# Experts ranked by token count: passes of two with 64 slots and of four with 32

## The reference

```python
N_EXPERTS, TOP_K, EXPERT_FF, SHARED_FF = 32, 4, 256, 512
comb = sum over the 4 chosen experts of one_hot(idx) * w        # (tokens, 32)
g = einsum("td,edf->tef", xf, w_exp_gate)                       # (32, 2048, 256)
u = einsum("td,edf->tef", xf, w_exp_up)                         # (32, 2048, 256)
a = silu(g) * u * comb
routed = einsum("tef,efd->td", a, w_exp_down)                   # (32, 256, 2048)
out = routed + (silu(xf @ w_sh_gate) * (xf @ w_sh_up)) @ w_sh_down
```

## Time and profile before

| | us |
|---|---|
| median of 3 runs | 1325.61 (1323.4 to 1325.62) |
| span of the profiled execution | 1322.1 |
| PE busy | 1222.6 (92%) |
| VectorE busy | 517.6 (39%) |
| ScalarE busy | 227.0 (17%) |
| moved by DMA | 379.59 MB, 287 GB/s over the span |

### The profile page before, as it was taken

The page is one execution under the profiler, slowest core; times in us unless marked ns, Lnnn a source line. Parts: engine busy times, 40 slices in busy tenths (PEclk is TensorE's granted clock), DMA queues, the critical chain, the costliest instruction groups (busy, mean ns, idle before and its releaser), DMA issues.

```text
span 1322.1 us, 16803 instructions
## 1 busy us (share of the span) xinstructions
PE 1222.6 (92%) x6125; PEld 655.8 (50%) x6126; DVE 517.6 (39%) x1058; ACT 227.0 (17%) x482; POOL 8.7 (1%) x13
## 2 busy tenths in 40 slices
PE   2789999999999899989979999999999999999974
PEld 0435588888744544457834444444334444444421
DVE  1200487656267588542532222222223332222215
ACT  4210200000125400040011111111111111111103
POOL 0000000000000000000000000000000000000001
PEclk9989999999999999989989999999999999999988
DMA  9999989996574499763549999945999999999951
GB/s 341 345 354 335 315 297 366 350 326 219 163 278 141 151 343 387 274 243 128 181 145 361 344 344 345 347 156 162 348 348 346 350 349 357 343 345 346 347 198 63
DMA packets 276337, 379.59 MB, mean 287 GB/s; under 512 B 12674, under 2 KB 182864, under 8 KB 274640
## 3 DMA queue, kind: packets, MB, share of 16 engines
q1 hardware_dynamic: 276304, 379.14, 84.1%
HBM read 377.01 MB, written 2.10 MB: 287 GB/s over the span
## 4 chain that ended last, share of the span: by engine, by line
PE 88%; DVE 3%; DMA 3%; issue 2%; SPq 2%; ACT 1%; POOL 0%; POOLq 0%; DVEq 0%; ACTq 0%
PE ps L485 85%; DMA ring<-in_w_mod 3%; DVE nreg L1619 1%; PE ps L855 1%; SPq L311 1%; PE ps L778 0%; SPq L303 0%; DVE tiny L1386 0%; PE ps L555 0%; DVE nreg L1623 0%; PE ps L730 0%; PE ps L872 0%; ACT nreg L928 0%; PE ps L500 0%; ACT nreg L1049 0%
## 5 line engine op out<-in xcount | busy, mean ns | idle before, releaser
L485 PE MATMUL ps<-nreg,ring 128*128 128x256 f32 (+1 forms) x1280 | 301.0, 395 | 10.2 <-ACT nreg L928 5.8
L485 PEld LDWEIGHTS ps<-nreg,ring 128*128 128x128 f32 x1280 | 244.0, 192 | 63.9 <-issue 21.8
L485 PE MATMUL ps<-ring,nreg 128*64 128x512 f32 x1088 | 241.2, 602 | 0.0
L1239 DVE SCALAR_TENSOR_TENSOR part<-ring,csT,part 128x512 f32<-128x512 f32 x240 | 180.4, 752 | 9.2
L1619 DVE TENSOR_TENSOR nreg<-nreg,ps 128x512 f32<-128x512 f32 x136 | 87.4, 684 | 176.2 <-PE ps L485 176.2
L485 PEld LDWEIGHTS ps<-ring,nreg 128*64 128x64 f32 x1088 | 77.5, 139 | 151.9 <-issue 151.9
L485 PE MATMUL ps<-nreg,conv 128*128 128x512 f32 x272 | 134.9, 618 | 13.5 <-DVE nreg L1619 13.5
L485 PE MATMUL ps<-ring,conv 128*64 128x512 f32 x544 | 128.0, 602 | 0.5 <-ACT conv L928 0.5
L485 PE MATMUL ps<-ring 128*128 128x512 f32 x256 | 110.8, 592 | 0.0
L485 PEld LDWEIGHTS ps<-nreg,conv 128*128 128x128 f32 x272 | 46.0, 189 | 101.5 <-DVE nreg L1619 60.2
L485 PE MATMUL ps<-pick,qnT 128*128 128x128 bf16 x544 | 93.2, 220 | 1.1 <-issue 0.6
(11 more groups left out here) (193 smaller groups left out, 753.1 us busy)
## 6 DMA issues: line engine op xcount, KB each, us to landing
ring<-in_w_mod SPq DMA_DIRECT2D x88, 1024.0 KB, 9.4
ring<-in_w_exp_gate SPq DMA_DIRECT2D x128, 512.0 KB, 8.2
ring<-in_w_exp_up SPq DMA_DIRECT2D x128, 512.0 KB, 8.6
ring<-in_w_exp_down SPq DMA_DIRECT2D x128, 512.0 KB, 8.6
ring<-in_w_in SPq DMA_DIRECT2D x15, 2048.0 KB, 11.9
ring<-in_w_out SPq DMA_DIRECT2D x8, 2048.0 KB, 10.9
ring<-in_w_mod SPq DMA_DIRECT2D x4, 2048.0 KB, 19.8
ring<-in_w_sh_up SPq DMA_DIRECT2D x2, 2048.0 KB, 10.2
```

Of the source, the lines that this page charges most:

```text
L485: return nc.tensor.matmul(o, l, r, start=start, stop=stop)
L1239: ins = V.scalar_tensor_tensor(out=acc, in0=w, scalar=scale, in1=acc, op0=ALU.mult, op1=ALU.add)
```

## The change

- VectorE and PE rank the experts by token count on the chip (`order`, largest first; ties by number). The counts are compared with each other expert's; a transpose and two matmuls permute places, weights and counts into ranked order. `order` is stored as integers, and SP reads the numbers of the experts of a pass into registers and loads their weights.
- The 16 heaviest experts go in 8 passes of two with 64 slots, the 16 lightest in 4 passes of four with 32 slots. The order is four rounds of: pair, pair, four. Each main pass has its own skipped or repeated `extra_passes` before it, so PE's loop over three rounds holds six pass bodies, and six stand behind it for the last round.
- In a pass of four the gate and up weights are eight units through four slots, the down weights four units through two slots.
- Channel order in the expert stage: chunk 4q + j, partition p is channel 512q + 4p + j. Four consecutive rows of gate and up weights lie in one partition, packets of 4 KB. Down weights are loaded in halves of 1024 columns, 4 KB too. The router and shared weights, the modulation columns, the norm's gain and the transposed tokens follow the same order: shared loads are four DMAs each, `bT2` and `fnT` are loaded apart in runs of four floats, `xh` is written from a strided read, and `mod_sum_cols` has a strided weight operand.
- The routing work moves in front of the split of the tokens on VectorE and among the first shared products on PE.

The core of the diff:

```diff
-        wg = w_exp_gate[0].rearrange("e (c p) n -> p e c n", p=P)
+        wg = w_exp_gate[0].rearrange("e (q p j) n -> p e q (j n)", q=4, j=4)
...
+            for at, src in ((bT2[:, 0:KC], b_mod[0, 3 * D:4 * D]), (bT2[:, KC:2 * KC], b_mod[0, 4 * D:5 * D]),
+                            (fnT[:, :], ffn_norm[0])):
+                sp.dma_start(at.rearrange("p (q j) -> p q j", q=4), src.rearrange("(q p j) -> p q j", q=4, j=4))\
+                  .then_inc(cols_in, 16)
...
+            def load_unit(v, q, experts):
+                for u, e in enumerate(experts):
+                    for g, src in ((0, wg), (1, wu)):
+                        sp.dma_start(gu[v][:, u, g, :, :].rearrange("p k n -> p (k n)"),
+                                     src[:, bass.ds(e, 1), q, :].rearrange("p a x -> p (a x)")).then_inc(gu_in[v], 16)
...
+            for i in range(ROUNDS):
+                quarters, halves = 12 * i, 6 * i
+                if i:
+                    for q in range(2, 4):
+                        sp.wait_ge(quarter_used, quarters - 2 + q // 3)
+                        load_unit(q, q, pair)
+                    for h in range(2):
+                        sp.wait_ge(half_used, halves)
+                        load_down(h, h, pair)
+                pair = [expert_at(4 * i + 2), expert_at(4 * i + 3)]
+                for q in range(4):
+                    sp.wait_ge(quarter_used, quarters + q + 1)
+                    load_unit(q, q, pair)
+                for h in range(2):
+                    sp.wait_ge(half_used, halves + h + 1)
+                    load_down(h, h, pair)
+                four = [expert_at(HEAVY + 4 * i + u) for u in range(4)]
+                for q in range(4):
+                    for g in range(2):
+                        v = 2 * q + g
+                        sp.wait_ge(quarter_used, quarters + (v + 5 if v < 4 else 8 + (v - 4) // 2 + 1))
+                        load_unit(v % 4, q, four[2 * g:2 * g + 2])
+                for g in range(2):
+                    sp.wait_ge(half_used, halves + g + 3)
+                    load_down(g, 0, four[2 * g:2 * g + 2])
+                if i + 1 < ROUNDS:
+                    pair = [expert_at(4 * i + 4), expert_at(4 * i + 5)]
+                    for q in range(2):
+                        sp.wait_ge(quarter_used, quarters + 11)
+                        load_unit(q, q, pair)
+                for g in range(2):
+                    sp.wait_ge(half_used, halves + 5)
+                    load_down(g, 1, four[2 * g:2 * g + 2])
...
+            def gate_up(units, use, wide, t, last):
+                for q in range(4):
+                    for g in range(units):
+                        v = units * q + g
+                        pe.wait_ge(gu_in[v % 4], 64 * use + 64 * (v // 4))
+                    pe.wait_ge((gx_act, gx_dve)[q % 2], 2 * t + (q // 2 + 1))
+                    for k in range(4):
+                        for u in range(2 * units):
+                            w = gu[(units * q + u // 2) % 4]
+                            ins = mm(ps[wide * u:wide * u + wide, 2, :], xg[:, 4 * q + k, wide * u:wide * u + wide],
+                                     w[:, u % 2, :, k, :], q == 0 and k == 0, q == 3 and k == 3)
...
-            with pe.Fori(0, NE // 2 - 1) as i:
-                extra_passes(i)
-                pair_pass(i, pe.snap(passes, min_val=0, max_val=64), True)
-                pe.reg_add(passes, passes, 1)
-            extra_passes(NE // 2 - 1)
-            pair_pass(NE // 2 - 1, pe.snap(passes, min_val=0, max_val=64), True, ahead=False)
+            with pe.Fori(0, ROUNDS - 1) as i:
+                for n in range(2):
+                    extra_passes(2 * i + n, PASSES - 1, 1, 4 * i + (n + 1))
+                    main_pass(1, 4 * i + (n + 1))
+                extra_passes(i + 8, NPASSES - 1, 2, 4 * i + 3)
+                main_pass(2, 4 * i + 3)
+            last_round = 4 * (ROUNDS - 1)
+            for n in range(2):
+                extra_passes(last_round // 2 + n, PASSES - 1, 1, last_round + n + 1)
+                main_pass(1, last_round + n + 1)
+            extra_passes(8 + ROUNDS - 1, NPASSES - 1, 2, last_round + 3)
+            main_pass(2, last_round + 3, ahead=False)
```

More of the change, by code:

```diff
@@ L70, in constants @@
     c[:, C_HALF] = -0.5
+    for p in range(P):
+        c[p, C_TIE:C_TIE + NE] = np.arange(NE) > p % NE
+        c[p, C_BLK + p // NE] = 1.0
+        c[p, C_EXP] = p % NE
+    c[:, C_OFF:C_OFF + NPASSES] = NARROW * np.arange(NPASSES)
     return c
@@ L131, in block_kernel @@
         xh = slot[3].rearrange("p (t d) -> p t d", t=2)
-        gu = ring[:, 0:16384].rearrange("p (q u g k n) -> p q u g k n", q=4, u=2, g=2, k=4)
-        down = [slot[4 + u].rearrange("p (k n) -> p k n", k=2) for u in range(2)]
+        gu = [slot[v].rearrange("p (u g k n) -> p u g k n", u=2, g=2, k=4) for v in range(4)]
+        down = [slot[4 + v].rearrange("p (u k n) -> p u k n", u=2, k=2) for v in range(2)]
+        tbl = vrow[:, :].rearrange("p (a e) -> p a e", a=4)
+        tblT = brow[:, :]
+        heavy = crow[:, :].rearrange("p (n t r) -> p n t r", n=PASSES, t=2)
+        blocks, sums = part[:, 1, 0:128], part[:, 1, 128:192]
         wkr = kq[:, 0:1024].rearrange("p (k n) -> p k n", k=KC)
@@ L847, in _ @@
-            gather(0, (2, 3))
-            def pair_pass(i, t, last, ahead=True):
+            for m in range(2):
+                shared_up(0, 0, sh_gate, m)
+            pe.wait_ge(mask_ready, 1)
+            mm(ps[:, 5, 0:32], before, mask[:, 0, :], True, True)
+            mm(ps[:, 5, 32:64], ones, mask[:, 0, :], True, False)
+            mm(ps[:, 5, 32:64], before, mask[:, 1, :], False, True)
+            mm(ps[:, 5, 64:96], ones, mask[:, 0, :], True, False)
+            mm(ps[:, 5, 64:96], ones, mask[:, 1, :], False, True).then_inc(rank_full, 1)
@@ new lines, in _ @@
+            shared_up(1, 2, sh_up, 0, range(8))
+            pe.wait_ge(sort_in, 1)
+            nc.tensor.transpose(ps[:, 6, 0:128], vrow[:, :], ident).then_inc(tbl_full, 1)
+            shared_up(1, 2, sh_up, 0, range(8, KC))
+            pe.wait_ge(tbl_out, 1)
+            mm(ps[:, 7, 0:128], tblT, blocks, True, True)
+            mm(ps[:, 7, 128:192], ones, sums, True, True).then_inc(sort_full, 1)
+            shared_up(1, 2, sh_up, 1)
+            pe.wait_ge(rank_ready, 1)
+            pe.wait_ge(sh_act, 2)
@@ L853, in pair_pass, with expert_pass @@
+            def expert_pass(units, use, t, last, ahead=True):
+                wide = P // (2 * units)
                 pe.wait_ge(pickw_ready, t + 1)
@@ L1587, in weighted_picks @@
[L1587 to L1592 removed]
+            heavy_slots = heavy.rearrange("p n t r -> p (n t r)")
+            light_slots = light[:, :, :, :].rearrange("p n t r -> p (n t r)")
```

353 lines of the change are left out of this document (203 added, 150 removed).

## The result

The changed kernel takes 1419.12 us (median of 4 runs, 1418.62 to 1421.12) against 1325.06 us (1323.4 to 1325.62): ratio 1.0716, 95% interval 1.0701 to 1.0732, slower by 94 us. The profiled execution took 1421.12 us with a span of 1419.3 (before 1322.1).

The account below looks back on a forecast made before the run. TensorE was taken to bound the kernel, the DMA nearly as full. Stage -26.2, stalls +92.4 and front +5.8 made +72.0 us; with the 1322.1 us span and 3.5 us around it 1398 us, range 1340 to 1420.

Parts of the forecast that it names:

- The stalls: TensorE's expert loop: 11 jumps over skipped repeats cost 8.4 us each, 6.2 idle plus slower clock; +92.4 us.
- the two jumps back: End of each turn of TensorE's new loop: between 0 and 6 us each, taken at nothing.
- The sign in the instruction queue: Profile after: the queue moves more packets than 22, by more than the added code.
- The reading of the two gaps: Kernel before, TensorE idle 6.83 us at loop entry, 5.82 behind it: jumps into code not held cost some 6 us.
- Rival (b): TensorE's jumps over a body cost nothing, the next code comes ahead of the jump: 1305 us, chance 0.20.
- The stage without stalls: Expert stage: nine passes of two 325.5 us, three fours of 70.0, a last of 65.8; 601.3 against 627.5, -26.2 us.
- Sum 70.0 us: A pass of four with a successor: 4.0 us to first request, 2.3 to bytes, ten units 51.1, then TensorE's remaining work.
- The front: Ahead of the expert stage: column loads, router packets, extra products, strided reads and weight loads; +5.8 us, range 0 to 13.
- the strided weight loads in the modulation sums: Front, eight groups of 8 records at 0.95 us each: between 0 and 7.6 us more, taken as 2.
- Rival (c): Packets don't matter, DMA stays at 349 GB/s: +34 us to any case, 1432 with the forecast; chance with (d) 0.05.
- Rival (d): The chip's ranking leaves a light expert with over 32 tokens; not in the sum, chance with (c) 0.05.
- SP's reads and VectorE's picks: Expert stage: SP's reads of 34 expert numbers and VectorE's 16 picks for a four are covered; nothing.

Follow-up runs that it names:

- experiment 3: The kernel before with TensorE's expert stage written straight, the repeat only ahead of the sixth pair, no skips: 1302.17 us, ratio 0.983.
- Experiments 9 and 10: experiment 3 with a test ahead of 13 later passes, jumping over a never-run body: 48 records in the first, 1301.86 us; 400 in the second, 1389.52 us.
- Experiment 1: The kernel before with TensorE's expert loop of two pass bodies written as a loop of four: 1450.88 us, ratio 1.096.
- Experiment 4: The changed kernel with TensorE's stage written straight, the repeat only ahead of the first pass, no skips: 1325.03 us, ratio 1.000.
- Experiment 5: Experiment 4 with the six ring slots given to gate/up and down units alike, in order of use: 1246.32 us, ratio 0.941.
- experiment 7: Experiment 4 with the channels laid out as in the kernel before, 1 KB packets for gate and up: 1332.64 us, ratio 1.007.
- experiment 8: experiment 3 with the experts' gate and up weights read in 4 KB packets, tokens not laid out to match: 1302.4 us.
- experiments 6 and 11: Experiment 5 plus a general second version with repeats, behind one test; TensorE reads eleven counts in the first, 1254.94 us, one VectorE sum in the second, 1244.03 us.

## Why the prediction was right

The forecast was 1398 us with 1340 to 1420, and the median is 1419.12: the direction and the cause held, and the time came out 21 us above the forecast. That it is still in the range is by 0.9 us, so partly luck: the stage's other errors all went one way.

- **The stalls: right in number, and by some luck in sum.** 11 x 8.4 = 92.4 us was the term, 94.1 is what taking the jumps out returned. Its parts were less exact. The idle time was 70.1 us against 11 x 6.2 = 68.2, but two errors meet in it: a jump ahead of a four costs 2.9 to 3.4 us and not 6.2, and the two jumps back, which I put at nothing, make their gaps 13.4 us, some 7 us more than a skip alone. The slower clock adds the rest. The sign in the instruction queue came too: the 8 bodies more (4160 records) are some 17 packets by the counts of experiment 3, an estimate, and the queue moved 45 more. Behind the gap at 763.91 the window of the changed kernel shows the same lower level as the earlier trace rows:
```profile
770.00:775.00 5.00, 4.54 (x12) 1.49 (x14) 1.75 (x8) 0.38 (x1) 0.00 (x0) 0.54 0.02 7
```
- **The reading of the two gaps, confirmed and made narrower.** That code which isn't at hand costs, and not the jump, was read from the earlier trace rows against the earlier trace rows. Experiments 9 and 10 show it directly, and show that it hangs on the distance. Rival (b), that the code behind a jump comes ahead of it, is true of 48 records and not of 400 or of a pass. (The pass period that the prediction gives as 36.17 us is 36.13 by its own two rows; nothing hangs on it.) The rule of the Trainium skill ("Runtime: NRT & Kernel Launch", Instruction fetch mechanics) is that a taken jump which lands outside what was prefetched waits for a fetch; experiments 9 and 10 agree with it. The same section gives TensorE's store 2048 instructions. Experiment 1 shows less: a loop of four bodies, 4 x 424 = 1696 matmul and weight-load records, isn't held. With the waits and register instructions beside them four bodies are some 1810 instructions, an estimate from experiment 3's 23 more packets for 13 more bodies, at 256 instructions a packet.
- **The stage without stalls: too optimistic by 17.7 us.** I had -26.2 us. Experiment 4 has 1307.74 - 688.72 = 619.0 us from the first gather's end to the last scatter's, against 627.5 before: -8.5. The failed term is a four, "Sum 70.0 us": the three with a successor take 72.8, 74.5 and 72.8 (+10.1 in all), the last 71.9 in place of 65.8 (+6.1), and the nine pairs 1.3 more in all. The rate was right, 410 to 412 GB/s. What was wrong is how many bytes go ahead of the last ones. In the first four of experiment 4 the last down weights were to land 57.4 us in (4.0 + 2.3 + 51.1); TensorE's products on them start 60.1 us in, and what follows takes 12.7 us, as in the sum (12.6):
```profile
842.63 0.35 SPq L448 DMA_DIRECT2D ring<-in_w_exp_gate  x1
...
856.64 3.64 PE L551 MATMUL ps<-ring,conv 128*32 128x512 f32 x16 [15.56 <-issue]
...
796.50:856.64 60.14, 28.91 (x266) 11.81 (x265) 7.55 (x21) 5.36 (x13) 0.00 (x0) 0.79 0.94 367
808.00:856.64 48.64, 21.53 (x199) 9.69 (x200) 4.45 (x11) 4.98 (x12) 0.00 (x0) 0.75 1.03 410
```
367 GB/s over 60.14 us are 22.07 MB, where ten units are 20.97. The 1.1 MB more are 2.7 us at 410 GB/s, all that is missing; SP issues the next pair's third and fourth quarters from 842.63 us on, while the last down units are still on their way, and the sum had left these out. In the last four three steps are longer: the first half's down weights come 1.7 us later, their products take 1.6 us more at the lower clock, and the last two down units 16.2 us in place of 12.5, with part of the final norm's gain among them. The end is 0.9 us shorter.
- **The pairs behind the fours.** They take 39.4 and 36.5 us in experiment 4, and part of it is not TensorE's own. Its gather waits for VectorE's picks, 2.05 us behind the first four and 0.58 behind the second:
```profile
885.61 0.29 PE L551 MATMUL ps<-pick,qnT 128*128 128x128 bf16 x1 [2.05 <-DVE pick L1717]
```
Ahead of these picks VectorE, whose program still has its loop and its skips, stands idle for 7.63 us at its loop's jump back and 4.23 us at the skip behind it, put down to no other engine. That it is the same stall as TensorE's is likely and not tested.
- **Where the gain of four passes fewer went.** Not into jumps alone. Without them the kernel still is no faster than before, because the fours wait for their weights: the ring holds half a four, and the pair passes before it can't load ahead, since slots are reserved, four for gate/up and two for down. Experiment 5 moved nothing but the slots and the order of the loads, and gained 78.7 us.
- **The front: 11.0 us by experiment 7 against 5.8.** The failed term is the strided weight loads in the modulation sums, of which I took 2 of 0 to 7.6 us. They went from 0.95 to 1.81 us for 8 records, eight times, 6.9 us, near the upper end. The Trainium skill, "SBUF — State Buffer", the note on cachelines, says that each access that crosses into a new 16-byte line pays; the trace agrees with it. The first of these sums starts at 191.9 us in experiment 4 and at 188.2 in experiment 7, where the layout is undone: 3.7 us, against the 2.7 at which the column loads were taken.
- **Rival (c)**, that packets don't matter, is wrong of the rate (experiment 7: 349 against 410 GB/s) and right of the pair passes (experiment 8).
- **Rival (d)** didn't occur: the trace has 13 passes and one repeat.
- **SP's reads and VectorE's picks**, taken at nothing: in the changed kernel's trace no gap of TensorE ahead of a gather is put down to them; the stalls cover what experiment 4 shows.

The span grew by 97.2 us where the sum said 72.0. The 25.2 between are the fours and the pairs (17.7), the front (the first gather ends 12.6 us later in place of 5.8) and the stalls (1.7), less 1.0 that I can't place. The forecast then added 3.5 us for what lies around the span; the changed kernel's median equals its profiled span within 0.2, so 21 us are left of the miss.

## What to carry to other kernels

TensorE's jump over code that it doesn't run was free over 48 records and cost 6.7 to 8.0 us on average over 400 and more, except in a loop of 848 records, which stayed at hand; so put rare work behind the common path in one block, with one test, and not ahead of each step. When passes alternate between two limits, here matmuls in a pair and transfers in a four, their sum counts only if the buffers can carry work across: give the slots out in order of use, and the average decides in place of the worst pass. A layout that makes packets larger pays only where the transfers set the pace (4 us a four, nothing in a pair), and its price falls on what reads the reordered data (11.0 us of the front).

## What the hardware did that I had not expected

- A jump back out of a long loop body adds to the skip behind it: 13.4 us in the changed kernel, 9.8 to 10.4 in the loop of four, where a skip alone costs 5.7 to 6.6.
- Skipping saves no fetches: 20 more instruction packets than in experiment 3 for 13 jumps over 400 records, as many as the skipped records fill.
- Reading one value from memory into a TensorE register takes about 0.68 us, with an addition, when eleven stand in a row (experiments 6 and 11); a single one ahead of each pass (experiment 9) adds nothing.
- The straight stage's pairs take 35.8 us where the held loop's take 36.1: 0.3 us a pass for loop, test and jump even where no gap of 6 us stands.
